# The first expert layer: token rows gathered by TensorE inside the block loop, where they went through DRAM

## The reference

```
for e in range(N_EXPERTS):
    act = jax.nn.silu(hf @ w_gate[e]) * (hf @ w_up[e])     # 1024 -> 512
    out = out + combine[:, e:e + 1] * (act @ w_down[e])    # 512 -> 1024
```

## Time and profile before

| | |
|---|---|
| median of three runs | 2602.76 us (2600.17 to 2603.2) |
| the profiled execution | 2601.16 us, its span 2599.5 us |
| PE busy, PE weight loads busy | 2256.3 us (87%), 1704.3 us (66%) |
| DVE, ACT, POOL busy | 1122.7, 545.6, 292.7 us |
| DMA | 637.78 MB, mean 245 GB/s |
| first experts (layer 0) | 361.7 to 650.9 us of the span |
| second, third experts | 1008.5 to 1472.7, 2095.1 to 2560 us |

### The profile page before, as it was taken

How to read it: one execution, slowest core, us unless ns; L and a number is a source line. 1 busy time by engine, 2 the same in 40 slices (tenths; PEclk the granted TensorE clock), 3 DMA queues, 4 the chain that set the end, 5 groups by cost and what they waited for, 6 DMA issues and landing times. The chain is left out here.

```text
span 2599.5 us, 87744 instructions
## 1 busy us (share of the span) xinstructions
PE 2256.3 (87%) x38076; PEld 1704.3 (66%) x38077; DVE 1122.7 (43%) x2768; ACT 545.6 (21%) x1187; POOL 292.7 (11%) x488
## 2 busy tenths in 40 slices
PE   8988977878999898777998889988889987887897
PEld 6876556667687645555776546777886565665674
DVE  5746342222563834222332366367764442222233
ACT  2244111111302711100111131043342111110111
POOL 1002132322100110000000100013334000000001
PEclk9999999999999999988999999989999999898999
DMA  8622189997413008999999911200003289999996
GB/s 336 248 89 106 50 306 402 378 386 300 164 67 130 1 19 347 428 429 428 427 396 428 369 65 65 81 11 4 3 5 132 82 340 428 429 428 428 428 407 242
DMA packets 92807, 637.78 MB, mean 245 GB/s; under 512 B 22757, under 2 KB 43497, under 8 KB 58618
## 3 DMA queue, kind: packets, MB, share of 16 engines
q1 hardware_dynamic: 48800, 586.71, 54.7%
q0 software_dynamic: 12752, 29.14, 3.5%
q10 hardware_dynamic: 31114, 19.86, 2.4%
HBM read 590.52 MB, written 45.12 MB: 245 GB/s over the span
## 5 line engine op out<-in xcount | busy, mean ns | idle before, releaser
L1491 PE MATMUL ps<-ring,arena 128*32 128x128 f32 x13056 | 402.6, 282 | 101.2 <-DMA ring<-in_experts 61.5
L1491 PEld LDWEIGHTS ps<-ring,arena 128*32 128x32 f32 x13056 | 374.1, 114 | 142.1 <-DMA ring<-in_experts 71.5
L1702 DVE TENSOR_TENSOR arena<-arena,ps 128x64 f32<-128x64 f32 x292 | 64.7, 221 | 565.3 <-ACT arena L1550 565.3
L1550 ACT ACTIVATE arena<-ps 128x64 f32<-128x64 f32 x292 | 65.2, 223 | 1054.4 <-PE ps L1491 927.1
L1502 PE MATMUL ps<-ring,arena 128*32 128x256 f32 x3264 | 203.7, 385 | 34.2 <-DVE arena L1705 21.0
L1468 PE MATMUL ps<-x_tok,arena 128*32 128x256 f32 x3456 | 219.2, 393 | 11.8 <-DVE arena L1605 8.4
L1491 PE MATMUL ps<-arena 128*32 128x128 f32 x5632 | 175.6, 284 | 44.3 <-DMA arena<-in_experts 33.5
L1491 PEld LDWEIGHTS ps<-arena 128*32 128x32 f32 x5632 | 162.4, 114 | 62.8 <-DMA arena<-in_experts 38.5
L1502 PEld LDWEIGHTS ps<-ring,arena 128*32 128x32 f32 x3264 | 104.3, 110 | 112.9 <-issue 30.7
L1441 PE MATMUL ps<-ring,arena 128*128 128x512 f32 x384 | 172.8, 606 | 3.4 <-PEq L2971 1.7
L1468 PEld LDWEIGHTS ps<-x_tok,arena 128*32 128x32 f32 x3456 | 119.4, 115 | 74.5 <-issue 25.6
(11 more groups left out here) (517 smaller groups left out, 3322.3 us busy)
## 6 DMA issues: line engine op xcount, KB each, us to landing
ring<-in_experts SPq DMA_DIRECT2D x165, 2048.0 KB, 24.9
arena<-in_experts SPq DMA_DIRECT2D x50, 2048.0 KB, 26.0
xt_mem<-in_experts SPq DMA_DIRECT2D x25, 2048.0 KB, 29.1
ring<-in_mixer_chunks SPq DMA_DIRECT2D x24, 2048.0 KB, 9.9
xybuf<-arena ACTq DMA_DIRECT2D x602, 32.0 KB, 7.0
xybuf<-arena SPq DMA_DIRECT2D x1, 9216.0 KB, 48.2
xbuf<-arena SPq DMA_DIRECT2D x1, 9216.0 KB, 70.1
arena<-xbuf POOLq DMA_DIRECT2D x168, 32.0 KB, 6.4
```

The costliest lines, as they stand in the source:

```text
L1491: ins = pe.matmul(ps[at, 2 + half, 0:P], xg[:, k, :], w_gu[half][:, k, q, :], start=(k == 0), stop=(k == NK - 1))
L1550: act.activation(silu_g[:, half, :], ps[:, 2 + half, 0:HALF], ACT.Silu).then_inc(s_silu[half], 1)
L1702: dve.tensor_tensor(hidden[:, half, :], silu_g[:, half, :], ps[:, 2 + half, HALF:P], ALU.mult)\
```

## The change

`sent` is set to False for the first layer too, so all that hangs on it goes:

```diff
             y_sb = take(AHEAD, D // 4)
-            sent = l == 0
+            sent = False
             if sent:
                 x_in = take(AHEAD, D // 4)
```

## The result

The changed kernel takes 2609.74 us (median of 13 runs, 2604.13 to 2615.66), the kernel before 2602.58 beside it (13 runs, 2599.3 to 2608.31): ratio 1.0023 [1.0014, 1.0032]. A second, equal set gave 2608.66 against 2602.08, 1.0024 [1.0013, 1.0035]. So the change costs 6 to 7 us, a little more than can be told from nothing, where 13.4 (2616.0 against 2602.58) had been forecast.

The account below looks back on a forecast made before the run. PE was taken to bound layer 1's dense stretch, while stores gave layer 0 slack; start -5.2, steps +17.4 and last block +1.5 make +13.7 us on 2601.16, 2614.9, predicted as 2616; eight-in-ten range 2609 to 2624.

Parts of the forecast that it names:

- The 41 steps: Layer 0's block-to-block steps on PE: at layer 1's step times 297.6 us, 300.9 with a slow first pass, from 283.51.
- the last block: Layer 0's last block, gate products to copy: 7.20 us with a gather inside instead of 5.69, 1.51 more.
- stalls persist: Rival: layer 0's stores stay as slow at the same places, giving 2624.6 us; chance 0.08, wholly or in good part.
- Hidden: Rival: stores set layer 0's pace, the gather fills PE's gaps, steps stay at 283.5 us; 2597.5 us, chance 0.06.
- The transfers set the pace: Rival: full DMA engines limit layer 0, so removing 5.8% of their time shortens it by 16.8 us; 2579, chance 0.03.
- The rule on weight loads: Skill's rule: PE's LDWEIGHTS share shows headroom; 64% in layer 0 would leave 2.5 us per step for the gather.
- the start: Ahead of layer 0's block loop: one gather instead of two, so the first gate products start 5.21 us earlier, at 356.51.
- the slow first pass: Layer 0's first loop pass: PE idles 3.27 us with no releaser, added in full to the changed kernel's steps.
- the base: The profiled execution of the kernel before, 2601.16 us, to which the forecast's terms were added.

Follow-up runs that it names:

- the gather added alone: Kernel before, rows still over DRAM, plus the change's gather in every layer 0 block, result unused: 2629.05 us, 1.0096 against before.
- the small stores in the kernel after: Changed kernel, but layer 0 stores only 8 of the 32 rows of each quarter of a block's result: 2610.12 us, 41 steps 300.08 us.

## Why the prediction was right in kind and too high

Right, with the size. The gather costs PE 1.50 us in every block and nothing hides it: but for four steps at the first passes and the end, they take 6.94 to 6.97, 7.59 to 7.64 and 8.09 to 8.17 us, as layer 1 had shown. The 41 steps took 300.27 and 299.20 against 300.9 forecast, and the last block 7.21 against 7.20. The waits for `xybuf` went altogether, so *stalls persist* is refuted. *Hidden* is refuted by the gather added alone, +25 to 27 us. *The transfers set the pace* is refuted by the small stores in the kernel after, unchanged. The rule on weight loads would have called 125.16 of 163 us (77%) a quarter of headroom; PE was busy 157.60 of them, at the steps of 6.95 that the forecast had as its floor.

The step that failed is *the start*, with the slow first pass that the sum charges to the steps: the idle times of the earlier trace rows were taken from one execution, and as the same with and without the scatter. Counted from the first one-hot, the sum made it 17.3 - 5.2 + 1.5 = 13.6 us, that is 3.7 less: 5.2 saved ahead of the loop, one gather more in block 0, and the slow first pass of 3.27 us charged to the changed kernel in full. It measured 11.2 and 10.9. The first part was right against this profile: the first gate products came 3.23 us after the one-hot, where 3.4 follows from the sum. The slow pass was not: block 0 took 7.98 us, where 6.94 + 3.27 = 10.21 had been put, so two thirds of that term were gone. The scatter put back into the changed kernel brings idle time at the start back, 7.08 us at once and 6 to 9 us in all; taken out of the kernel before, it leaves 1.52 us ahead of the down products and a start of 13.7. Over all profiles the start takes 16.5 to 28.2 us in the ten with the scatter and 10.9 to 13.7 in the four without.

The other half of the error is in the base. The profiled execution had the shortest start of three, 17.3 against 18.1 and 25.4, mean 20.3. I had read 3.27 us ahead of the down products off one execution, and the next two idled 4.93 and 3.62 there, the first of them also 4.7 us longer ahead of its second gather. With 20.3 before and 11.05 after, the start gives 9.2 us where the forecast had 3.7: 5.5 us, 3.0 of them by the base and 2.5 by the first pass. The steps behind it, the last block included, grew by 18.7 where the forecast had 17.4: 1.3 the other way. That leaves +9.5 us of stage against +13.7 forecast.

Open: the medians are 7.2 and 6.6 us apart, not 9.5, and the time lies below the forecast's own range (2611 to 2619) and only just inside the wide one (2609 to 2624). That it is inside is luck: no bound of it allowed for a base with a start of 20 us. The other stages' sums differ by 1.5 us on the mean of three and two profiles, which is no more than their scatter. With them the profiled executions are 8.0 us apart on the mean, within the interval of the ratio (3.6 to 8.3 us). Whether the lost scatter (4 MB) helps outside the stage as well isn't settled.

What rested on a reason that fell: the prediction named GpSimd's transfers as work "on an engine that PE does not wait for". PE doesn't wait for the scatter's data, true; it was held up beside it as traffic, in idle time that no row attributes to it.

## What to carry to other kernels

Where a change takes traffic away, look at the idle times without a releaser (`issue`) near the place where that traffic runs: no edit on the engine itself touches them, and they can still go with the traffic. Look there for the transfers of instructions among the DMA queues too. Read a stall whose length comes from contention in two or three executions before it enters a sum, and price the steady loop and its start apart. A copy of the loop that already runs in another layer is worth more than any price list: here it gave 41 steps to within 2 us.

## What was not expected of the hardware

PE's idle time in the first pass of the loop goes with the traffic on GpSimd's queue, and in one of the two places the trace shows what it ends with. Ahead of the first block's down products PE idles 0.51 to 0.81 us in the changed kernel (that queue at 8% of the DMA time between 340 and 375 us), 1.52 in the kernel before without its scatter (17.7%), and 3.27, 4.93 and 3.62 in the kernel before (44 to 45%). In these profiles one transfer of 16 KB on a queue of instructions lands 1.4 to 1.6 us before PE goes on, as here in the second profile of before (372.5 to 374) and in after (358.5 to 360):

```profile
q8 instruction: 1, 0.02, 3.7%
```

```profile
q8 instruction: 1, 0.02, 4.2%
```

It lands at 373.70 and PE goes on at 375.16, 1.46 us later; after the change at 359.56 and 361.08, 1.52 later. It starts 6.5 and 3.7 us after the gate products. So PE waits there for code, which comes later while the scatter runs. That is read from the times alone: the queue doesn't name the engine that it serves, and the trace doesn't say why the transfer starts late. The other place, the late signal to VectorE's first transpose, stands in six of the ten profiles with the scatter, where VectorE idles 3.2 to 6.0 us ahead of it, and in none of the four without. No transfer of instructions goes with it throughout, and what holds it is open.

Idle time on PE can cost twice. Ahead of three of the down products that waited for the silu in the kernel before, the products after the wait ran slower, at first. One of them, with the earlier trace rows as the case at full clock:

```profile
430.64 2.83 PE L1502 MATMUL ps<-ring,arena 128*32 128x256 f32 x32 [2.15 <-DVE arena L1705]
433.57 4.35 PE L1491 MATMUL ps<-ring,arena 128*32 128x128 f32 x128
```

That is 2.83 and 4.35 us of busy time against 1.97 and 3.68 at the full clock, 1.5 us more. The clock had fallen (PE, PEld, DVE, ACT, POOL busy, then the granted clock):

```profile
430.60:433.50 2.90, 2.83 (x32) 1.10 (x32) 0.79 (x3) 1.51 (x2) 0.96 (x2) 0.66 1.03 412
```

It is 0.83 over the next 4.4 us, and 1.00 ahead of the two and behind them. Three such places, behind waits of 2.15, 2.26 and 2.31 us, make 4.6 us of busy time in layer 0; the waits of 2.32 us at 481.14 and of 2.29 us at 600.30 cost nothing of the kind, at a clock of 1.00. Over 361 to 651 us the granted clock was 0.98, 0.96 and 0.96 before, and 1.00 in both profiles after, where no product inside the loop waits so long.

One store of 128 KB over 4 x 32 rows made copies wait up to 16.7 us for it, where four stores of 32 KB on the same queue made them wait 4.8 us at most. The long waits let the clock fall too: the down products at 459.08, behind 12.47 idle us, take 3.64 us, with a granted clock of 0.50 over 459.0 to 462.8.
